# Reordering the second attention's loads, dot products and scale rows, and halving V blocks, in a one-core streaming encoder step

## The reference

```python
sh1, sc1, g1, sh2, sc2, g2 = modulation(c, w_ada, b_ada)       # from a vector per sequence
h = rmsnorm(x, norm1_g) * (1 + sc1) + sh1
za, zg, q, k, v = split(h @ w_in)
y_conv = silu(layernorm(causal_dwconv(za * sigmoid(zg))))       # width 31
o = attn_fn(q, k, v)                                            # 16 heads of 64, banded, relative bias
x = x + g1 * (concat(y_conv, o) @ w_out)
h2 = rmsnorm(x, norm2_g) * (1 + sc2) + sh2
# retrieval: per token 8 heads x top 16 of 128 x 128 experts, so 128 picks per token
u, vv = u_tab[eidx], v_tab[eidx]                                # rows of 2048 values
act = gelu(einsum('td,ted->te', h2, u))
x = x + g2 * einsum('te,ted->td', g * act, vv)
y = rmsnorm(x, final_g)
```

## Time and profile before

| | |
|---|---|
| median of 3 runs | 3911.17 us (3910.19 to 3914.08) |
| the profiled execution's own time | 3912.98 us |
| its span in the profile | 3911.2 us |
| PE busy | 3659.4 us (94%) |
| DVE busy | 2665.0 us (68%) |
| ACT busy | 444.2 us (11%) |
| POOL busy | 1022.0 us (26%) |
| moved by DMA | 1418.49 MB, mean 363 GB/s |

### The profile page before, as it was taken

How to read it: one execution, slowest core, us unless ns; L and a number is a source line. 1 busy time by engine, 2 the same in 40 slices (tenths; PEclk the granted TensorE clock), 3 DMA queues, 4 the chain that set the end, 5 groups by cost and what they waited for, 6 DMA issues and landing times.

```text
span 3911.2 us, 34419 instructions
## 1 busy us (share of the span) xinstructions
PE 3659.4 (94%) x12521; PEld 1929.5 (49%) x12521; DVE 2665.0 (68%) x4253; ACT 444.2 (11%) x975; POOL 1022.0 (26%) x888
## 2 busy tenths in 40 slices
PE   5899999998998898899989999999998899999996
PEld 2566545476543663466734444444465344444443
DVE  1258853157888788878986777767688754555666
ACT  2100004110000440102600000000052000000000
POOL 1000001215324344343232222222233322222331
PEclk8999999998999799999999999999999999999998
DMA  9878773559999899999799999999989999999997
GB/s 387 274 247 275 256 290 128 198 204 405 413 414 417 331 379 413 395 406 361 266 415 421 414 411 422 421 419 418 417 294 358 421 421 380 421 422 422 421 417 310
DMA packets 337760, 1418.49 MB, mean 363 GB/s; under 512 B 26009, under 2 KB 134529, under 8 KB 195742
## 3 DMA queue, kind: packets, MB, share of 16 engines
q0 software_dynamic: 120752, 848.17, 53.8%
q1 hardware_dynamic: 215840, 563.29, 37.8%
q10 hardware_dynamic: 1008, 4.98, 0.3%
HBM read 1390.84 MB, written 47.28 MB: 368 GB/s over the span
## 4 chain that ended last, share of the span: by engine, by line
DMA 50%; PE 31%; issue 12%; DVE 5%; POOL 2%; ACT 1%; DVEq 0%; POOLq 0%; SPq 0%; ACTq 0%
DMA R<-in_u_experts,MS 36%; DMA R<-in_v_experts,MS 10%; PE bank L895 8%; PE bank L926 7%; PE bank L1119 4%; PE bank L1298 3%; DMA R<-in_w_ada 2%; DVE R L2321 2%; PE bank L840 1%; POOL R L776 1%; DVE R L2201 1%; PE bank L1294 1%; PE bank L812 1%; PE bank L1183 1%; DMA R<-in_w_in 1%
## 5 line engine op out<-in xcount | busy, mean ns | idle before, releaser
L776 POOL DMA_INDIRECT R<-in_u_experts,MS x640 | 817.9, 1278 | 1699.1 <-DVE MS L2201 1477.7
L2201 DVE CUSTOM_DVE_ANT_0 R<-R 128x2048 f32<-128x2048 f32 x374 | 856.6, 2291 | 383.3 <-DMA R<-in_u_experts,MS 361.8
L1328 PE MATMUL bank<-R,RB 128*128 128x512 f32 x2304 | 1024.6, 603 | 48.2 <-DMA R<-in_v_experts 48.2
L1328 PE MATMUL bank<-RB 128*128 128x512 f32 x1792 | 778.2, 592 | 0.0
L1328 PEld LDWEIGHTS bank<-R,RB 128*128 128x128 f32 x2304 | 443.1, 193 | 619.6 <-issue 559.1
L2201 DVE CUSTOM_DVE_ANT_0 R<-R,RB 128x2048 f32<-128x2048 f32 x266 | 608.6, 2288 | 124.2 <-DMA R<-in_u_experts,MS 123.4
L1328 PEld LDWEIGHTS bank<-RB 128*128 128x128 f32 x1792 | 340.5, 190 | 428.6 <-issue 428.6
L2321 DVE SCALAR_TENSOR_TENSOR R<-R,MS 128x2048 f32<-128x2048 f32 x128 | 301.5, 2355 | 198.1 <-DMA R<-in_v_experts,MS 197.7
L895 PE MATMUL bank<-RB,R 128*128 128x256 f32 (+1 forms) x1536 | 399.8, 421 | 23.2 <-DMA R<-in_w_pq 18.8
L895 PEld LDWEIGHTS bank<-RB,R 128*128 128x128 f32 x1536 | 294.0, 193 | 122.6 <-DMA R<-in_w_pq 19.3
L1119 PE MATMUL bank<-RB,R 128*128 128x384 f32 x1024 | 334.9, 487 | 10.1 <-DMA R<-in_w_in 8.8
(11 more groups left out here) (355 smaller groups left out, 2248.5 us busy)
## 6 DMA issues: line engine op xcount, KB each, us to landing
R<-in_v_experts SPq DMA_DIRECT2D x144, 1024.0 KB, 9.1
RB<-in_v_experts SPq DMA_DIRECT2D x112, 1024.0 KB, 9.1
R<-in_w_ada SPq DMA_DIRECT2D x48, 2048.0 KB, 14.0
R<-in_w_in SPq DMA_DIRECT2D x20, 2048.0 KB, 18.8
R<-in_w_in SPq DMA_DIRECT2D x24, 1024.0 KB, 33.4
R<-in_w_out SPq DMA_DIRECT2D x8, 2048.0 KB, 8.4
R<-in_w_pq SPq DMA_DIRECT2D x8, 2048.0 KB, 10.6
R<-in_w_out SPq DMA_DIRECT2D x16, 1024.0 KB, 33.0
```

The costliest lines, as they stand in the source:

```text
L776: pool.indirect_dma_start(dst, None, table, bass.IndirectOffsetOnAxis(ap=expert[T_ % 2][:, c:c + 1], axis=0)).then_inc(signal, 16)
L1328: x = pe.matmul(PB[4 * h + q][:, :], W[:, i, h * P:(h + 1) * P], vring[slot][:, q * PW:(q + 1) * PW], start=(i == 0), stop=(i == NKEY - 1))
L2201: V.tensor_tensor_reduce(u, u, x, 1.0, 0.0, ALU.mult, ALU.add, dots[t % 2][:, h * TOPK + s:h * TOPK + s + 1]).then_inc(dots_done, 1)
```

## The change

Seven edits:

- SP: block 6 (w_out, first 512 columns) is no longer loaded between the two halves of the V rows' stores, ahead of the attention, but at head 3, behind that head's bias rows and the values of pair 1.
- SP: the scale rows A2Y and n2Y go behind w_out's block 8 instead of block 7; B2Y[0] goes behind block 9 instead of 8. n2Y signals the same semaphore as A2Y.
- VectorE: `steps(16)` becomes `steps(20)`; the `steps(2)` after v = 9 and the two single dots beside the norms are gone. A2Y is worked on at v = 7 instead of v = 4.
- TensorE: `stay_busy` at head 0 is 34 matmuls instead of 22, and two new ones stand before head 1's scores.
- ScalarE: exp and gelu of tile 1 stand before the thirteenth of the 16 query copies, not behind all of them.
- SP and TensorE: V blocks 0 to 17 of each pass are loaded as two column halves (128 rows of 4 KB, 0.5 MiB each) with a semaphore for each half; TensorE goes through columns 0 to 1023 of a block, then 1024 to 2047. The half of block i + 2 may be loaded when that half of block i is used.
- Two semaphores of the scale rows are merged into others.

```diff
         s_lnv, s_lnr, s_lnx, s_cat = (sem(n) for n in ("ln_var", "ln_sqrt", "ln_x", "cat_ready"))
-        s_x5, s_g1, s_sc2, s_sh2 = sem("x_again"), sem("g1_in"), sem("sc2_in"), sem("sh2_in")
+        s_x5, s_g1, s_sc2, s_sh2 = sem("x_again"), sem("g1_in"), sem("sc2_and_n2g_in"), sem("sh2_in")
...
+        v_half = [sem(f"v_right_half_{i}") for i in range(2)]
...
         NBAT = 2 * P // 4
+        NUSE = NKEY + VLATE
...
             values_out(0)
-            load_block(6, "w_out", 0)
             values_out(1)
...
                 if b == 1:
                     values(hp)
+                if h == 3:
+                    load_block(6, "w_out", 0)
...
             for b in range(7, 10):
                 load_block(b, "w_out", (b - 6) * PW)
-                if b == 7:
+                if b == 8:
                     spread(A2Y, 1, s_sc2)
-                    sp.dma_start(n2Y, n2rows_d[:, :]).then_inc(s_n2, 16)
-                if b == 8:
+                    sp.dma_start(n2Y, n2rows_d[:, :]).then_inc(s_sc2, 16)
+                if b == 9:
                     sp.wait_ge(s_A2, 3)
                     sp.dma_start(B2Y[0], modrows_d[2, 0]).then_inc(s_sh2, 16)
...
-                for i in range(NKEY):
-                    if i < 2:
-                        sp.wait_ge(oh_used, NBAT * pair + NBAT - 1 + i)
-                    else:
-                        sp.wait_ge(vp_used, NKEY * pair + v_free(i))
+                for i in range(VLATE):
+                    for c in range(2):
+                        if i < 2:
+                            sp.wait_ge(oh_used, NBAT * pair + NBAT - 1 + i)
+                        else:
+                            sp.wait_ge(vp_used, NUSE * pair + 2 * (i - 2) + c + 1)
+                        at = slice(c * 2 * PW, (c + 1) * 2 * PW)
+                        sp.dma_start(vring[i % 2][:, at], v_tab[i * P:(i + 1) * P, at]).then_inc((v_half if c else v_piece)[i % 2], 16)
+                for i in range(VLATE, NKEY):
+                    sp.wait_ge(vp_used, NUSE * pair + v_free(i) + min(v_free(i), VLATE))
                     slot, _ = v_slot(pair, i)
...
+                if h == 1:
+                    stay_busy(5, 2)
                 pe.wait_ge(mx_ready, NH + h)
...
                 if h == 0:
-                    stay_busy(5, 22)
+                    stay_busy(5, 34)
...
             def dense(pair):
                 pe.wait_ge(w_read, NBAT * (pair + 1))
-                for i in range(NKEY):
+                for i in range(VLATE):
+                    for c in range(2):
+                        pe.wait_ge((v_half if c else v_piece)[i % 2], 16 * (pair * (VLATE // 2 if c else per_slot(i % 2)) + i // 2 + 1))
+                        for h in range(2):
+                            for q in range(2 * c, 2 * c + 2):
+                                x = pe.matmul(PB[4 * h + q][:, :], W[:, i, h * P:(h + 1) * P],
+                                              vring[i % 2][:, q * PW:(q + 1) * PW], start=(i == 0), stop=False)
+                        x.then_inc(vp_used, 1)
+                for i in range(VLATE, NKEY):
                     slot, landed = v_slot(pair, i)
...
             def keep_queries(G, dst, tiles):
                 for n in range(16):
+                    if G and n == 12:
+                        gate_exp(1)
+                        gelu(1)
                     act.wait_ge(q_done, 16 * G + n + 1)
...
-            gate_exp(1)
-            gelu(1)
             copy_turned(0)
...
-            steps(16)
+            steps(20)
...
-                if v == 4:
-                    dve.wait_ge(s_sc2, 16 * 2)
-                    dve.wait_ge(s_n2, 16)
+                if v == 7:
+                    dve.wait_ge(s_sc2, 16 * 3)
                     for b in range(2):
                         STT(out=A2Y[b], in0=A2Y[b], scalar=1.0, in1=n2Y, op0=ALU.add, op1=ALU.mult).then_inc(s_A2, 1)
                 if v < 3 * TY:
                     steps(4)
                 elif v == 3 * TY:
-                    steps(2)
                     dve.wait_ge(s_A2, 3)
                     dve.wait_ge(s_sh2, 16)
                 elif v < 4 * TY:
                     norm_tile(TX + v - 3 * TY - 1, A2Y[0], B2Y[0])
-                    steps(1)
```

More of the change, by code:

```diff
@@ L298, in hybrid_encoder_step @@
         s_lnv, s_lnr, s_lnx, s_cat = (sem(n) for n in ("ln_var", "ln_sqrt", "ln_x", "cat_ready"))
-        s_x5, s_g1, s_sc2, s_sh2 = sem("x_again"), sem("g1_in"), sem("sc2_in"), sem("sh2_in")
-        s_x5x, s_g1x, s_sc2x, s_sh2x, s_n2x = (sem(n) for n in ("first_x_again", "first_g1_in", "first_sc2_in", "first_sh2_in", "first_n2g_in"))
+        s_x5, s_g1, s_sc2, s_sh2 = sem("x_again"), sem("g1_in"), sem("sc2_and_n2g_in"), sem("sh2_in")
+        s_x5x, s_g1x, s_sc2x, s_sh2x = (sem(n) for n in ("first_x_again", "first_g1_in", "first_sc2_and_n2g_in", "first_sh2_in"))
         o_done, o_free = sem("wout_done"), sem("wout_free")
@@ L356, in v_slot, with per_slot @@
         def v_slot(pair, i):
-            if i < VLATE:
-                slot, use = i % 2, i // 2
-            else:
-                slot = (i - VLATE + 2) % 4
-                use = (i - VLATE) // 4 + (VLATE // 2 if slot < 2 else 0)
-            per = (NKEY - VLATE) // 4 + (1 if (slot - 2) % 4 < (NKEY - VLATE) % 4 else 0) + (VLATE // 2 if slot < 2 else 0)
-            return slot, 16 * (pair * per + use + 1)
+            slot = (i - VLATE + 2) % 4
+            use = (i - VLATE) // 4
+            return slot, 16 * (pair * per_slot(slot) + (VLATE // 2 if slot < 2 else 0) + use + 1)
+        def per_slot(slot):
+            return (VLATE // 2 if slot < 2 else 0) + (NKEY - VLATE) // 4 + (1 if (slot - 2) % 4 < (NKEY - VLATE) % 4 else 0)
         def v_free(i):
-            if i < VLATE:
-                return i - 1
             return 8 * (i - VLATE + 1) if i < VLATE + 2 else i - 3
@@ L617, in _ @@
                 if pair == 1:
-                    sp.wait_ge(vp_used, NKEY - 3)
+                    sp.wait_ge(vp_used, NUSE - 3)
                     pick_values_in(2)
@@ L751, in _ @@
                     dma(B2X, rows(mod_d, [[0, P]], D, 3 * D)).then_inc(s_sh2x, 16)
-                    dma(n2X, rows(ins["norm2_g"].tensor, [[0, P]], D)).then_inc(s_n2x, 16)
+                    dma(n2X, rows(ins["norm2_g"].tensor, [[0, P]], D)).then_inc(s_sc2x, 16)
             pool.wait_ge(pv_done, NH)
@@ L1328, in dense @@
                             x = pe.matmul(PB[4 * h + q][:, :], W[:, i, h * P:(h + 1) * P],
-                                          vring[slot][:, q * PW:(q + 1) * PW], start=(i == 0), stop=(i == NKEY - 1))
+                                          vring[slot][:, q * PW:(q + 1) * PW], start=False, stop=(i == NKEY - 1))
                             if pair == 1 and i == NKEY - 1:
@@ L1623, in drain @@
             def drain():
-                act.wait_ge(vp_used, NKEY)
+                act.wait_ge(vp_used, NUSE)
                 for h in range(2):
@@ L1937, in _ @@
                 if v == 3:
[L1938 to L1939 removed]
+                    dve.wait_ge(s_sc2x, 32)
                     STT(out=A2X, in0=A2X, scalar=1.0, in1=n2X, op0=ALU.add, op1=ALU.mult).then_inc(s_A2, 1)
```

7 lines of the change are left out of this document (2 added, 5 removed).

## The result

The changed kernel took 3930.34 us (median of 9 runs, 3918.49 to 3938.13), the kernel before beside it 3911.17 us (9 runs, 3902.68 to 3926.06): ratio 1.0037, 95% interval 1.0022 to 1.0053. It is slower by 0.37%, where I had forecast 3895 us (range 3866 to 3914) and faster. A ratio here is always that of the fast executions, and can lie up to 0.12% beside the quotient of the two medians; one execution of e14 took 6806.1 us at a mean granted clock of 0.714 and is in no ratio. The profiled execution took 3933.1 us, its span is 3931.3.

What follows compares the result with a forecast made beforehand. Chain half DMA, a third PE; DMA engines full at 414 to 419 GB/s through the dense passes, VectorE setting the w_out stage. Terms -8 - 7.5 - 7 + 9 - 4 - 0.5 + 2 = -16 gave 3895 us, range 3866 to 3914.

Steps and rivals of the forecast that it cites:

- The dots, -8: Attention's start: with w_out's 4 MiB gone, at most 12.6 us of VectorE's gather waits go; 8 us saved.
- The bias wait, -7.5: Head 0: bias rows no longer behind w_out in SP's queue, so head_max comes earlier; 7.5 us saved.
- heads 1 to 3, -7: Attention: longer TensorE cover keeps the clock up; three heads at 8.1 us instead of 10.5 save 7 us.
- Head 4, +9: Attention: head 4's bias rows behind the four w_out loads; w_out gets 155 GB/s, mask 9 us late.
- rival C: Dense passes: turns by packet give V half rows a smaller share, 9.3 us a block; 3908 us, chance 0.12.
- w_out and the norms, -4: VectorE after attention: four dots ahead +14.8, shorter stretch behind v = 9 -13, fewer gather waits -6; 4 us faster.
- The gate values, -0.5: Gate weights: VectorE's 8.0 us stand for ScalarE's exp was cover, so moving exp and gelu saves 0.5 us.
- The halves, +2: Dense passes: V done 25 us early, then gathers run alone at VectorE's pace; 2 us slower over two passes.
- the wait at build(1): After dense(0): TensorE, finished earlier, waits 15 us or more for VectorE's rows.
- D: Attention, held SP list: head 4's rows 44 us late or more, 33 us of stall; 3930 us, chance 0.10.

Runs made afterwards that it cites:

- e14: Repeat of e4: the kernel before with four dots moved ahead of w_out's first group and scale rows later; 1.0019 (1.0000 to 1.0038).
- e4: Kernel before, with only four dots taken ahead of w_out's first group and the scale rows' loads and multiplication moved later; 1.0027, 3923.13 us.
- e7: Kernel before, with only the four dots moved ahead of w_out's first group, scale rows left in place; 1.0000 (0.9988 to 1.0013).
- e9: e5 with TensorE's covering matmuls as in the kernel before (22 and none); 0.9999 (0.9986 to 1.0011), 3913.21 us.
- e11: Changed kernel, with w_out's first block in four single loads behind heads 5, 7, 9 and 11 instead of behind head 3; 1.0000 (0.9990 to 1.0010).
- e3: Kernel before, with only w_out's first block moved behind head 3 and TensorE's longer covering matmuls; 1.0003 (0.9990 to 1.0017).
- e5: Kernel before, with w_out's first block in four single loads behind heads 5, 7, 9 and 11, and TensorE's longer cover; 0.9973, 3909.62 us.
- e16: Repeat of e5: the kernel before with w_out's first block in quarters and TensorE's longer cover; 0.9990 (0.9973 to 1.0007), median 3907.67 us.
- e10: Kernel before, with only the gate's exp and gelu moved ahead of ScalarE's thirteenth query copy; 0.9996 (0.9981 to 1.0010).
- e1: Kernel before, with only the first 18 V blocks of each dense pass in column halves; 1.0015 (0.9998 to 1.0033), 3918.85 us.
- e15: Kernel before, with V column halves in dense(1) alone; 1.0008 (0.9989 to 1.0027), median 3915.59 us.
- e8: Kernel before, with V column halves in dense(0) alone, dense(1)'s blocks loaded whole; 0.9991 (0.9979 to 1.0002).

## Why the prediction was wrong

The four parts by measured ratio: block 6 +0.03%, dots and rows +0.27 and +0.19%, gate values -0.04%, halves +0.15%; with the middle of the second, 0.37%, which is the whole. Each is uncertain by some 0.15%, so the sum by some 0.3%: that it meets the whole so closely is luck, and what it says is that the parts roughly add up. I had forecast -16 us; these come to +14. Three steps failed: the dots at the attention's start, the cost at head 4, and the norms behind w_out; a fourth, the halves, was mis-sized. Step by step, all against dot 0 and from the traces:

- *The dots, -8.* They came 1.6 us sooner by dot 123. This step failed. With w_out's 4 MiB out of the stage the DMA engines moved 397 GB/s for 415 (1205 to 1265 us), but the gather waits stayed, 10.9 us for 20 dots (1210 to 1270.9 us) where the earlier trace rows have 12.6 for 21. I had taken it that the room would go to the gathers, but the engines were no less full (DMA share 1.00 for 1.02): in those 60 us the gathers' queue moved 19.39 MB for 18.85. At the end of the stage the gathers nearly fill the engines alone; from 1261 to 1272 us, after:

```profile
q0 software_dynamic: 545, 3.94, 95.8%
```

- *The bias wait, -7.5, and heads 1 to 3, -7.* Right in kind: dots 123 to 124 lost 5.8 us, and heads 0 to 3 8.6 of 31.6. The first is less firm than it looks, for in e4 and e7, which leave the block where it was, those two dots are as close (9.5 us) with dot 123 2 and 5 us late. Over all executions dot 124 starts 418.6 to 421.3 us behind dot 0 in the nine kernels with the block moved, and 422.9 to 426.9 in the nine without: this step and the one above gave 7.4 us together here, and 2 to 8 over all pairs, for 15.5. e9, where heads 0 to 3 take 36.3 us, supports that TensorE's cover is needed for the second.
- *Head 4, +9.* This step failed in its size, twice. Between heads 3 and 4 lie 24.3 us for 8.3 before, 16.0 more. I had given w_out what the gathers leave of 415 GB/s, 155. In the trace the two queues take turns by packet, and with rows of 2 KB against 8 KB w_out got 87 GB/s while gathers were due; 35.1 us passed from its first issue to head 4's rows, for my 27. My rival C had that very rule, from the earlier trace rows, and I did not use it here. I had also left out the keys and values that lie in the same queue: it moved 6.94 MB in those 35.1 us, and w_out is 4.2 of them. And I had not priced the clock that falls when TensorE stands: from head 4's `head_max` to head 15's are 92.7 us, 4.0 more, all of it at heads 5 and 6. Together +20 for +9. With the dots' miss that makes -13.5 into +4.0. That it is this placement, not the move, that ate the gain, e11 shows against the changed kernel, with intervals apart (1.0000 and 1.0037, measured on different chips); e3 against e5 says the same, e3 against e16 is within the noise.
- *w_out and the norms, -4.* From dot 155 to v = 9 the changed kernel needs 15.1 us more, which is my +14.8; the -6 of gather waits never came (35.1 us for 56 dots, 31.5 for 52). Behind v = 9 I took off 13 and 7.7 came: three waits of 6.0 us (0.33 of them seen before) had been covered by the dots that I counted as a saving. This step failed too. I had named the cover of B2Y's wait and overlooked that of ScalarE and of the x1 store. +7.3 in the trace. What remains open is its price in time: the pair measured 1.0027 and 1.0019 (from 1.0009, and from 1.0000), the dots alone and the rows alone no slower (up to 1.0013 and 1.0007), so whether it takes both is not settled. In the stage itself the two add up, 4.2 and 2.0 us for the 6.5 of e4.
- *The gate values, -0.5.* Right, as far as e10's interval of some 0.15% can tell.
- *The halves, +2.* The reason was right, that V is then through early and VectorE sets the pace; so was the wait at build(1), 14.74 us without a loss. The size was off: nothing in dense(0), where dots are still to come that use the freed bytes, and 4 to 6 us in dense(1) by the traces of e1 and e15. By time this is less certain: 1.0015, 1.0008, and 0.9991 without it.

Of the rivals, D named the right place and a like time, but by a stall of 33 us that wasn't there: 16.8 us at head 4 were enough, because the dots and the norms failed as well. That its 3930 us is what was measured is luck. C's unequal turns did not come. Between 1960 and 2060 us the V queue and the gathers' had 3886 and 3787 packets, one for one though half as long, and 7.5 us a block where I had worked out 7.6 for that case. The Trainium skill ("DMA: Bandwidth & Descriptors", section "Queues, rings and completion order") has the engines take the queues in turn, a packet at a time, and the trace agrees. The halves gained share all the same: the V queue moved 11.97 MB in those 100 us before and 14.17 after. Before, it had 1638 packets to the gathers' 4063, so with whole blocks it was probably empty between two of them; that is argued, not shown.

## What to carry to other kernels

Do not put a long load into the list of a queue that feeds a tight ring: one load at a time between the ring's own, and look at whether TensorE's clock survives the wait that is left. Price a load beside gathers by packets and not by the bytes that they seem to leave: here a row of 2 KB took a turn against one of 8 KB, 87 GB/s for the 155 that I had worked out. Before work is taken from between two dependent steps, list what they wait for besides that work; a wait of 0.33 us in the trace (for ScalarE's square root) was one of 1.17 without its cover, and one that the trace did not show at all (for the store of x1) was 3.10. Where bytes are the bound, a faster consumer only moves them; it costs where it leaves another engine alone at the end. And lay traces side by side from an event behind the part that nobody changed, since here dot 0 alone moved by 19 us.

## What I had not expected of the hardware

The attention is unsteady by itself, and most of it goes with TensorE's granted clock. In e8 and e14, which change nothing there, the stage came out 6.0 and 6.9 us longer: the clock was at 0.50 from 1300 to 1320 us in both and only at 0.79 and 0.90 in the 20 us behind, where it was at 0.57 and 1.00 before. In e4, the same kernel as e14, the stage was 4.7 us shorter and the clock back at 0.79 and 1.00, but 3.8 of the 4.7 were there by dot 124, where head 0 waited 2.67 us for its bias rows and not 9.49. The shorter cover of e9 measured 0.09% above e16 and 0.26% above e5; the intervals overlap, so that it costs time is seen in its trace, and not shown by its times.
